# First layer's entry rebuilt: x loaded first, squares added on VectorE, modulation used tile by tile inside the key and value pair

## The reference

```
mod_x = silu(c) @ w_ada[i] + b_ada[i]            # and mod_c from c_ctx, for the context tokens
sh1, sc1, gt1, sh2, sc2, gt2 = split(mod_x, 6)   # 1024 values each
hx = rmsnorm(x, g_pre1[i]) * (1 + sc1) + sh1     # hc the same for the context tokens
ux = hx @ w_in[i]                                # keys and values are two of its column blocks
k_all, v_all = concat([kc, kx]), concat([vc, vx])
```

## Time and profile before

| | |
|---|---|
| median of 3 runs | 2218.48 us (2216.47 to 2219.58) |
| the profiled execution: its own time | 2219.41 us |
| its span, first to last instruction | 2217.6 us |
| PE busy | 2129.1 us (96%), PEld 1805.5 (81%) |
| DVE, ACT, POOL busy | 1340.1 (60%), 793.2 (36%), 784.1 (35%) us |
| mean granted TensorE clock | 0.985 |

### The profile page before, as it was taken

How to read it: one execution, slowest core, us unless ns; L and a number is a source line. 1 busy time by engine, 2 the same in 40 slices (tenths; PEclk the granted TensorE clock), 3 DMA queues, 4 the chain that set the end, 5 groups by cost and what they waited for, 6 DMA issues and landing times.

```text
span 2217.6 us, 27943 instructions
## 1 busy us (share of the span) xinstructions
PE 2129.1 (96%) x11302; PEld 1805.5 (81%) x11302; DVE 1340.1 (60%) x1814; ACT 793.2 (36%) x1152; POOL 784.1 (35%) x359
## 2 busy tenths in 40 slices
PE   6999999999999999999999989899999999999997
PEld 6877788888888888888888877778777877888885
DVE  6469899855874687847616665889854352101113
ACT  2447612233324523222212345662244353222223
POOL 3320023232335433323323346103444465444442
PEclk9999999999999999999999989999999999999998
DMA  7110011132344143533323222002222332233321
GB/s 298 48 38 1 15 53 58 42 120 86 124 149 141 65 127 130 190 100 128 112 79 113 92 90 93 30 1 80 84 84 90 122 97 87 94 95 95 95 86 67
DMA packets 63200, 205.24 MB, mean 93 GB/s; under 512 B 7136, under 2 KB 8288, under 8 KB 62816
## 3 DMA queue, kind: packets, MB, share of 16 engines
q1 hardware_dynamic: 57744, 190.87, 26.7%
q10 hardware_dynamic: 5328, 12.59, 1.5%
HBM read 197.79 MB, written 5.64 MB: 92 GB/s over the span
## 4 chain that ended last, share of the span: by engine, by line
PE 78%; DVE 16%; ACT 2%; DMA 1%; issue 1%; POOL 1%; ACTq 0%; DVEq 0%; SPq 0%
PE ps L534 71%; DVE conv_acc L1644 3%; DVE ps L1644 2%; DVE unit_stats L1605 2%; PE ps L560 2%; DVE pt0l L1625 1%; DVE pt1l L1625 1%; DVE probs L1619 1%; PE ps L597 1%; PE ps L744 1%; PE ps L578 1%; DMA w_raw<-in_w 1%; PE ps L618 1%; PE ps L588 1%; POOL w_l L430 1%
## 5 line engine op out<-in xcount | busy, mean ns | idle before, releaser
L430 POOL TENSOR_TENSOR w_l<-w_raw,w_h 128x1024 fp32r<-128x1024 f32 (+3 forms) x296 | 684.5, 2317 | 1280.6 <-ACT w_h L901 1280.4
L534 PE MATMUL ps<-h_h,w_h 128*128 128x512 f32 (+1 forms) x1296 | 427.9, 370 | 8.2 <-ACT t L1159 4.2
L534 PE MATMUL ps<-h_l,w_h 128*128 128x512 f32 (+1 forms) x1296 | 425.0, 368 | 0.0
L534 PE MATMUL ps<-h_h,w_l 128*128 128x512 f32 (+1 forms) x1296 | 424.6, 368 | 0.0
L901 ACT ACTIVATE w_h<-w_raw 128x1024 fp32r<-128x1024 f32 (+3 forms) x296 | 280.5, 950 | 227.4 <-PE ps L534 148.8
L534 PEld LDWEIGHTS ps<-h_h,w_h 128*128 128x128 f32 x1296 | 243.6, 189 | 58.4 <-ACT t L1159 6.6
L534 PEld LDWEIGHTS ps<-h_h,w_l 128*128 128x128 f32 x1296 | 244.7, 189 | 43.4
L534 PEld LDWEIGHTS ps<-h_l,w_h 128*128 128x128 f32 x1296 | 244.2, 188 | 42.1 <-issue 1.2
L1499 DVE CUSTOM_DVE_ANT_0 ps<-ada_raw,c_row 128x1024 f32<-128x1024 f32 x160 | 268.0, 1675 | 9.5 <-DMA ada_raw<-in_ada 4.5
L534 PE MATMUL ps<-f_h,w_h 128*128 128x258 f32 (+1 forms) x672 | 173.1, 339 | 0.9 <-DVE t L1830 0.9
L534 PE MATMUL ps<-f_h,w_l 128*128 128x258 f32 (+1 forms) x672 | 173.5, 340 | 0.0
(11 more groups left out here) (244 smaller groups left out, 3224.3 us busy)
## 6 DMA issues: line engine op xcount, KB each, us to landing
w_raw<-in_w SPq DMA_DIRECT2D x222, 512.0 KB, 3.6
ada_raw<-in_ada SPq DMA_DIRECT2D x80, 512.0 KB, 3.7
w_raw<-in_w SPq DMA_DIRECT2D x50, 256.0 KB, 3.2
ada_first<-in_ada SPq DMA_DIRECT2D x16, 512.0 KB, 6.6
w_raw<-in_w SPq DMA_DIRECT2D x16, 384.0 KB, 3.1
x<-in_x ACTq DMA_DIRECT2D x8, 384.0 KB, 17.5
x_again<-in_x ACTq DMA_DIRECT2D x8, 384.0 KB, 8.7
x_between<-x SPq DMA_DIRECT2D x8, 384.0 KB, 2.3
```

Of the source, the lines that this page charges most:

```text
L430: nc.gpsimd.tensor_tensor(wl[:, s % RING, 0:n], raw[:, s % RAW, 0:n], wh[:, s % RING, 0:n], ALU.subtract).then_inc(split, 1)
L534: ins = nc.tensor.matmul(at(out, c0, c1), w[:, s % RING, b * P:(b + 1) * P], m[:, kt, first + c0:first + c1], start=(kt == 0 and n == 0), ...
```

## The change

All of it lies in the entry of layer 1, but for the size of the key and value slabs, which are now loaded, rounded and split as 4 blocks and not as 8 in the first loads of layer 1 and in layer 2.

- DMA order: SyncE issues x tiles 0 to 5 first, then the first two modulation tiles, slabs 0 and 1, ten more modulation tiles (12 places now), slabs 2 and 3, the last four modulation tiles and last the block of `const` with the head mask, edges and rotary tables (`tables_loaded`). ScalarE's queue issues `cvec`, `vec`, the first 256 columns of `const` and x tiles 6 and 7. `c_row` is no longer loaded.
- Sum of squares: ScalarE squares all 8 tiles into `norm_tmp`; VectorE adds them (7 adds); TensorE does one set of token sums.
- silu(c) is copied to all partitions on TensorE (`spread_c`, 16 fp32 products of 128 columns into PSUM), and VectorE copies it from PSUM to `c_row`; the first dots read it from PSUM.
- Products on zeros (`fill`) run on TensorE before, between and after these.
- The pair (`first_pair`) has six of the eight shift tiles between its steps. VectorE goes tile by tile: two dots, a gain for that tile, and x times the token factor of a later tile, in place. ScalarE writes for each tile `h_h` and, by a second pass, the unrounded value into `norm_tmp`; GpSimd subtracts for all eight tiles.
- The context part of the values lies beside the keys in PSUM and is copied out after ScalarE has read the keys.

```diff
-ADA_SLOTS = 6
+ADA_SLOTS = 12
 def slab_blocks(s):
+    if s < S_Q:
+        return 4
@@ SyncE
-            sp.dma_start(c_row[:], io["c_row"]).then_inc(c_row_loaded, 16)
-            load(0, KT)
-            load(1, KT)
...
+            for k in range(KT - 2):
+                sp.dma_start(x[:, k, :], io["x"][:, k, :]).then_inc(x_loaded[k], 16)
+            load_first(0)
+            load_first(1)
+            load_run(0, 2)
+            for n in range(2, ADA_START):
+                if n == ADA_SLOTS:
+                    load_run(2, RING)
+                load_first(n)
+            sp.dma_start(const[:, C_BLK:NC], io["const"][:, C_BLK:NC]).then_inc(tables_loaded, 16)
@@ GpSimd
             split_run(0, 2)
-            for k in range(1, KT, 2):
-                add_squares(0, "pre1", 0, k)
+            lows(0, "pre1", 0, range(2))
             split_run(2, RING)
-            lows(0, "pre1", 0)
+            lows(0, "pre1", 0, range(2, 6))
+            split_run(RING, RING + 1)
+            lows(0, "pre1", 0, range(6, KT))
@@ TensorE
+            pe.wait_ge(*seen("blank"))
+            fill(3, LAT)
+            pe.wait_ge(const_loaded, 16 * 2)
             pe.wait_ge(*seen("silu"))
-            for k in range(0, KT, 2):
-                shift_tile(k)
-                shift_tile(k + 1)
-                square_sum(0, "pre1", 0, k)
+            spread_c()
+            fill(3, LAT)
+            pe.wait_ge(*seen("sq_sum", KT - 1))
+            token_sums(scaled_tile(0), 0, "pre1").then_inc(*pe_done.up("stat", 0, "pre1"))
+            fill(1, CTX)
+            spread(0, "pre1", 0, "pre1", w=1, to=at(A[1], 0, T))
+            shift_tile(0)
+            shift_tile(1)
+            pe.wait_ge(*seen("free", "spread", 0, "pre1"))
+            fill(2, LAT)
+            def first_pair(s):
...
+                    n = {("high", 0): 2}.get((kind, k), k + 3 if kind == "low" else KT)
+                    if n < KT:
+                        shift_tile(n)
@@ ScalarE
+            def first_high():
+                act.wait_ge(*seen("spread", 0, "pre1"))
+                nc.scalar.activation(t1[:, 0:T], at(A[1], 0, T), ACT.Copy).then_inc(
+                    *act_out.up("free", "spread", 0, "pre1"))
+                rounds(1)
...
+                shift(0)
+                for k in range(KT):
+                    act.wait_ge(*seen("shift", k))
+                    act.wait_ge(*seen("gain", k))
+                    act.wait_ge(*seen("xn", k))
+                    modulated(hh[:, k], k, act_hi, "hh", 0, "pre1", k)
+                    if k + 1 < KT:
+                        shift(k + 1)
+                    modulated(scaled_tile(k), k, act_tmp, "t", 0, "pre1", k)
+                    if k in (1, 5, 6):
+                        rounds({1: RING - 1, 5: RING, 6: RING + 1}[k])
@@ VectorE
+            total = scaled_tile(0)
+            for k in range(1, KT):
+                dve.wait_ge(*seen("sq", k))
+                link(v.tensor_tensor(total, total, scaled_tile(k), ALU.add), dve_tmp, "sq_sum", k)
...
+            for k in range(KT):
+                scale_tile(k)
+                for n in ((0, 1), (2,), (3,), (4,), (5,), (6,), (7,), ())[k]:
+                    by_token_factor(n)
```

More of the change, by code:

```diff
@@ L338, in key_rows @@
             return out if n == P else out.rearrange("p k (r q) -> p k r q", q=P)
[L341 to L353, removed]
+        pool_last, pool_adds = (0, 2, 4, 6), (4, 6)
         def scaled_tile(n):
@@ L571, in keep_warm @@
                     nc.tensor.matmul(psf[:, 512:1024], wh[:, s % RING, 0:P], wh[:, s % RING, 0:512], start=True, stop=True)
+            def first_pair(s):
+                steps = []
+                for k in range(KT):
+                    steps += [("high", k)] + ([("low", k - 1)] if k else [])
+                steps.append(("low", KT - 1))
+                for i, (kind, k) in enumerate(steps):
+                    sa = s + 2 * (k // 4)
+                    b = k % 4
+                    if kind == "high":
+                        if b == 0:
+                            pe.wait_ge(split, sa + 2)
+                        pe.wait_ge(*seen("hh", 0, "pre1", k))
+                    else:
+                        pe.wait_ge(*seen("hl", 0, "pre1", k))
+                    first, last = i == 0, i == len(steps) - 1
+                    for n, (w, m) in enumerate(((wh, hh), (wl, hh)) if kind == "high" else ((wh, hl),)):
+                        for c0, c1, ctx_part in chunks(0):
+                            ins = nc.tensor.matmul(at(A[1], c0, c1), w[:, sa % RING, b * P:(b + 1) * P], m[:, k, c0:c1],
+                                                   start=first and n == 0, stop=last and not ctx_part)
+                    if kind == "low" and b == 3:
+                        ins.then_inc(used, 1)
+                    for n, (w, m) in enumerate(((wh, hh), (wl, hh)) if kind == "high" else ((wh, hl),)):
+                        for c0, c1, ctx_part in chunks(0):
+                            ins = nc.tensor.matmul(value_piece(0, c0, c1), w[:, (sa + 1) % RING, b * P:(b + 1) * P],
+                                                   m[:, k, c0:c1], start=first and n == 0 and not ctx_part, stop=last)
+                    if kind == "low" and b == 3:
+                        ins.then_inc(used, 1)
+                    n = {("high", 0): 2}.get((kind, k), k + 3 if kind == "low" else KT)
+                    if n < KT:
+                        shift_tile(n)
@@ new lines, in fill, with spread_c @@
+            def fill(n, cols):
+                for _ in range(n):
+                    nc.tensor.matmul(psf[:, 1536:1536 + cols], t2[:, 0:P], t2[:, 0:cols], start=True, stop=True)
+            def spread_c():
+                for s in range(2):
+                    for b in range(KT):
+                        ins = nc.tensor.matmul(c_spread(s)[:, b * P:(b + 1) * P],
+                                               silu_c[:, b, s:s + 1].to_broadcast([P, P]), ident, start=True, stop=True)
+                ins.then_inc(*pe_done.up("c_spread"))
@@ L1536, in _, with by_token_factor @@
+            def by_token_factor(k):
+                dve.wait_ge(*seen("free", "spread", 0, "pre1"))
+                v.tensor_tensor(x[:, k, :], x[:, k, :], t1[:, 0:T], ALU.mult).then_inc(*dve_out.up("xn", k))
+            for k in range(KT):
+                scale_tile(k)
+                for n in ((0, 1), (2,), (3,), (4,), (5,), (6,), (7,), ())[k]:
+                    by_token_factor(n)
+            noted[("free", "c_spread")] = noted[("ada", ADA_START - 1)]
             for ly in range(LAYERS):
```

209 lines of the change are left out of this document (95 added, 114 removed).

## The result

The changed kernel takes 2200.35 us, the median of 4 runs (2197.6 to 2202.75), beside 2219.03 for the kernel before on the same chip (4 runs, 2216.47 to 2222.15). The ratio is 0.9915, with a 95% interval of 0.9895 to 0.9935: faster by 18.7 us.

What follows compares the result with a forecast made beforehand. TensorE's one long chain bounds the kernel, so the pair's end decides: 68.6 instead of 80.59 is 12.0 earlier, less 1.2 lost behind it, 10.8; from the median 2218.48 that gives 2207.6 us, range 2197 to 2215.

Steps and rivals of the forecast that it cites:

- The drain of 1.38: ScalarE's squares: a possible drain behind the table load, left out of the sum; with it, 1.4 later.
- I take half of the way: Pair on TensorE: mean of full and half rate, start 31.4, length 39.7, less 2.5, so end 68.6.
- mixed case: Pair's clock between full and half rate, 3 to 6 steps at half: 2202 to 2214, chance 0.60.
- the full-rate case: Rival: full rate throughout the entry, VectorE the bound, pair ends at 59.8, gain 19.6, time 2198.9; chance 0.20.
- the port: Rival in the pair: x products meet GpSimd and dots slow down; pair ends at 68 to 77, 2212; chance 0.07.
- So of 3.83 only the product is exposed: VectorE's tile in the pair: only the x product is slowed beside GpSimd, 0 to 1.6 us, six times.
- the 1.5 of the sum: VectorE in the pair: total allowance for x products delayed by GpSimd, moving its end from 58.3 to 59.8.
- VectorE's 59.8: Pair's end by VectorE's path: gain 7 at 53.2, 5.1 behind it, and 1.5 for GpSimd.
- My 56: Pair's end by TensorE at full rate: start 27.7 plus length 28.2.
- The warning on the rounding of slab 5: ScalarE in the pair: slab roundings of 1.04 cost nothing unless ScalarE exceeds 3.8 a tile, making high(6) and high(7) late.
- The gap of 2.2 us: TensorE behind the pair: context values wait for ScalarE's key reads; gap 2.2, not 1.03, so 1.2 lost.
- everything after is one TensorE chain, so it passes on whole: Program behind the pair: the 10.8 won there reaches the kernel's end undiminished.

Runs made afterwards that it cites:

- e1: Changed kernel without any of its four sets of products on zeros; 2204.60 us, ratio 0.9944.
- e3: Changed kernel without the context sample's scale dot, its scale copied from the other sample, so one dot a tile; 2206.73 us, ratio 0.9951.
- e5: Changed kernel with each tile's two-column gain computed by two one-column instructions; 2203.33 us, ratio 0.9931.
- e6: Changed kernel with two products on zeros in TensorE's gap behind the pair; 2202.93 us, ratio 0.9926.
- e7: Changed kernel with one-column gains, two products on zeros in the gap behind the pair, and slab 5 rounded behind the last tile; 2199.16 us, ratio 0.9907.
- e10: e7 with ScalarE writing a tile before, not after, it copies the next shift; 2203.18 us, ratio 0.9926.
- e11: e10 without the two products on zeros right ahead of the pair; 2207.77 us, ratio 0.9954.
- e12: The changed kernel itself run again, nothing altered; 2203.77 us, ratio 0.9935.
- e9: Changed kernel without the last two products on zeros, right ahead of the pair; 2209.38 us, ratio 0.9961.
- e8: Kernel before the change with six dense products of 512 columns added ahead of the pair; 2216.93 us, ratio 0.9986.

## Why the prediction was right, and where it was wrong

**Right.** The pair's end decides, and what is won there is passed on. The steps, by their own numbers:

| step | predicted | measured |
|---|---|---|
| squares' adds end | 18.1 | 16.1 |
| factors | 21.7 to 24.3 | 21.3 |
| gain of tile 0 | 25.4 | 22.1 |
| pair starts | 27.7 to 35 | 28.4 |
| gain of tile 7 | 53.2 to 55 | 55.0 |
| TensorE's full-rate step with a shift tile | 4.0 | 3.9 |
| pair's end at full rate | 59.8 by VectorE, 56 by TensorE | 60.93 |
| gap behind the pair | 2.2 | 2.1 |

The adds end two early because `const` landed at 7.44 and the squares began at 7.6, not 9.6: the table load that I put behind the constants ran while they came in. ScalarE in the changed kernel, timeline:

```profile
3.25 1.28 ACT L1079 ACT_TABLE_LOAD   x1 [3.25 <-issue]
4.55 0.22 ACT L1079 ACTIVATE silu_c<-cvec 128x16 f32<-128x16 f32 x1
4.78 1.28 ACT L1009 ACT_TABLE_LOAD   x1
7.46 0.20 ACT L1009 ACTIVATE spare<-const 128x1 f32<-128x1 f32 x1 [1.39 <-DMA const<-in_const]
```

The second load now starts right behind silu's ACTIVATE and ends at 6.06, before the constants are there. The drain of 1.38 that the Trainium skill (ScalarE: Activation LUTs, What ACT_TABLE_LOAD costs) adds to a load does not show in these rows: the first load ends at 4.53 and its ACTIVATE starts 0.02 later, and the second load starts 0.01 behind that ACTIVATE. Here the measurement decides, and leaving the drain out of the sum was right.

**Wrong: "I take half of the way".** This is the step that failed. It put the pair's end at 68.6 by taking the mean of two rates for its start and its length; measured is 60.93, 7.7 earlier. The full rate came at 31.7, in the pair's first step, and stood until 62.4, through six shift tiles of 1.7 to 1.84. I knew rows for both sides, one of half-busy work that held the full rate and one of tiny work alone that never got it, and I took the mean of the two. That mean is right only where the rate comes up midway. All kernels with shift tiles in the pair held it to the pair's end once it was up there (the change, e1, e3, e5, e6, e7, e10, e11, e12 and, from 51.9 on, e9). What can go the other way is when it comes up, and e9 shows that as the forecast's mixed case: slab at 70.99, 2209.38. The two products on zeros bring it in the first step; I had listed them and given them only the cost of their columns. By the rule of the Trainium skill that I weighed there (TensorE: Matmul & The Clock Gate, HAM oscillation) the clock would have fallen at every tile. That rule is told of waits, and shift tiles are work, if tiny: between dense steps 1.7 us of shift tile apart the clock did not fall, but in the 2.1 us gap behind the pair, with waits of 1.48 and 0.81 in the 6 us before it, it did.

So it is partly luck that the time fits. The likeliest case as I had it spanned 2202 to 2214, and 2200.35 lies in the range only because the range took in the full-rate case, to which I gave 0.20. That it stands 1.5 from that rival's 2198.9 is no exact hit either: the pair ended 1.1 later than the rival says, the slab behind it cost 2.75 that nobody had, and by the medians 2.9 came back later in the program.

**Mis-placed: the port.** "So of 3.83 only the product is exposed" named the wrong instruction. The first two products took 2.90 us together beside a split, 1.0 more than twice 0.95, and the six later ones 0.95 each; the wait fell on the gain, which I had at 0.2. It is 0.29 alone and 1.75, 0.93, 1.77 and 2.44 beside GpSimd. VectorE and then GpSimd in the timeline of the change, same moment:

```profile
52.60 2.44 DVE L1593 TENSOR_SCALAR gain<-mod,scale_b,vec 128x2 f32<-128x2 f32 x1
...
52.60 2.41 POOL L445 TENSOR_TENSOR w_l<-w_raw,w_h 128x1024 fp32r<-128x1024 f32 x1
```

A gain of two columns lasts until GpSimd's subtraction of 1024 is done; each of the four ended within 0.03 us of the GpSimd instruction beside it. The four excesses make 5.7 us in all and the first two products 1.0, against the 1.5 of the sum. But gain 0 came 3.3 early, and a tile without a wait took 3.58 and not 3.83, so gain 7 still fell at 55.0: errors that offset each other. The Trainium skill says it (SBUF — State Buffer, Who interferes with whom): tensor_scalar can take the pair of ports that GpSimd needs, and whoever comes second waits for the whole instruction. The trace agrees with that, with the durations just given. The dots stayed at 1.21 and 1.22 beside GpSimd, as forecast from PSUM as one operand.

**Right in size, wrong in reason: the bound.** I had VectorE's 59.8 against 56 for TensorE, and 60.93 seems to say VectorE. The timeline of ScalarE in the change says otherwise:

```profile
53.11 0.26 ACT L986 ACTIVATE mod<-ps,vec 128x2 f32<-128x2 f32 x1 [0.29 <-PE ps L638]
53.27 1.30 ACT L991 ACTIVATE norm_tmp<-x,mod,gain 128x256 f32<-128x256 f32 x2
54.47 1.04 ACT L961 ACTIVATE w_h<-w_raw 128x1024 fp32r<-128x1024 f32 x1
55.42 1.29 ACT L991 ACTIVATE h_h<-x,mod,gain 128x256 fp32r<-128x256 f32 x2
```

ScalarE waits for TensorE's last shift tile (it ends at 53.07), and from there works without a pause: the shift's copy, the value of tile 6, the rounding of slab 5, and only at 55.42 tile 7, whose gain is there at 55.04. So the pair's end was TensorE's even steps to 53.07 and 7.9 us behind them. My 56 had the steps right (start 28.4, 3.9 each) and left that tail out, which I had charged to VectorE's path alone. VectorE is 0.4 us from being the bound, so the chain's row by row account could name either; e3 and e5, which relieve VectorE, keep the tail at 7.8 us, and e10, which shortens the tail, runs into VectorE. The warning on the rounding of slab 5 held, in small: it is in this tail, and e7, which moves it and has the single-column gains too, has the slab 0.5 earlier than e6.

**Missed: the rate behind the pair.** The gap of 2.2 us was in the sum at 1.2; that it also costs the clock was not. The slab after it pays 2.75 us, more than the gap's own growth. e6 shows that this is the gap's doing, since two products on zeros in it remove it.

**Missed: the rest of the program.** I had "everything after is one TensorE chain, so it passes on whole". In the profiles the start of a late TensorE instruction (one at 1305.0 before) is 18.4 us earlier in the change, and the end 21.8. Work after the entry is the same, yet the clock falls at other places. The border of the layers, TensorE, in the change and then in e12, the same kernel:

```profile
1298.10:1301.30 3.20, 3.20 (x32) 1.00 0.01 3
1301.50:1308.00 6.50, 4.87 (x17) 0.50 0.42 167
```

```profile
1298.10:1301.30 3.20, 3.20 (x17) 0.50 0.01 3
1301.50:1308.00 6.50, 6.50 (x27) 0.50 0.31 121
```

Up to 1286 us the two agree to 0.1; in the first of these stretches one has the full clock and 32 instructions, the other half the clock and 17, and they end 4.0 apart. So about 4 us of a single profile belong to no edit, and what e6 and e7 had won by the second slab (2.5 and 3.1) is smaller than that. With the parts put together: 7.7 of the span's error of 11.0 (2206.8 forecast, 2195.8 measured) are the mixed rate, 2.75 go the other way behind the pair, 6.0 come from the falls later on. That the later falls are chance is shown for e12 against the change. For 2.0 of the 6.0 the record points the same way: the kernel before fell to half rate at 425.1 and the change's profile did not, while e1, e6 and e10, with the changed kernel's program there, fell at the same place (412.3, 407.0, 407.7). That the whole 6.0 is chance was not shown.

No version here is clearly better than the changed kernel: e7's 2199.16 is 1.2 under one set of its runs and 4.6 under the other, and the intervals of the ratios overlap.

## What to carry to other kernels

Tiny TensorE work (loads of weights for two columns) is cheap between dense products and dear in a row: here six shift tiles cost 3.59 each in a row, 3.93 with the wait for ScalarE between them, and 1.7 inside the pair. Moving them was worth 14.2 us at the first query slab, some of it because ScalarE's work on the tiles then ran beside them and not behind. Dense products right ahead of the stretch whose rate matters paid here in both kernels (e8, e9); in the gap behind it they paid 2.5 us in the profile (e6), which the medians don't show. Read the rate from the distance of equal products, not from the mean clock. When a sum has two rates, forecast each and give it a chance instead of the mean; and before you shorten one engine's chain, work out for each engine its last step and all that must follow it, since here two such ends lay 0.4 us apart.

## What was not expected of the hardware

- A VectorE tensor_scalar of 128x2 lasted up to 2.44 us beside a GpSimd subtraction, but the same of 128x1 never more than 0.276 (16 of 16 in e5 and in e7, eight of those in e7 wholly inside a GpSimd instruction).
- The granted clock held 1.00 from 31.7 to 62.4, the first 21 us of it 2.2 us of dense work and 1.7 us of two-column products in turn, and with the same mixture took until 36.9 (e1) or 51.9 (e9) to come up. Two such shift tiles alone, ahead of the pair, saw it fall (24.9).
- At the start of the program the profile's clock can't be trusted: it gives 1.00 for the first 66 us of the kernel before, where the distances are those of half rate up to there.
- Equal runs of one kernel take their clock falls at different places, 4.0 us apart at the end (the change and e12).
